# Three latent projections placed between the last normalisation's sums, later ones by token block, weight buffers rotated by one

## The chip, the core and the metric

One core of a Trainium2 chip runs the whole program. The metric is the device time of one execution in microseconds (us); for a kernel it is the median of several runs. TensorE does the matrix products, VectorE, ScalarE and GpSimd the elementwise work, SyncE issues the DMAs.

## The reference, cut to what matters

The program is a two-layer decoder trunk on 1024 tokens of width 1024. Each layer is a token mixer and a gated ConvFFN, each with an RMSNorm before it and one behind it. The change lies where layer 0's feed-forward ends and layer 1's mixer (DSA) begins:

```
def rms_norm(x, g):  y = x * rsqrt(mean(x*x) + eps);  return y * g
for i in range(2):
    x = x + rms_norm(mixer_i(rms_norm(x, g[i,0])), g[i,1])
    y = conv_ffn(rms_norm(x, g[i,2]), ...)
    x = x + rms_norm(y, g[i,3])
# layer 1's mixer:
proj = h @ w_in          # h = rms_norm(x, g[1,0]); w_in gives q, c, qi, ki, wi
c = rms_norm(c, kv_norm) # c: the latent, 256 wide
k = rope(c @ w_uk);  v = c @ w_uv
ki = rope(ki)            # the indexer's key, 64 wide; wi: 8 wide
```

So between the two layers stand two normalisations one behind the other: the "post" norm of the feed-forward's output, added to x, and the "pre" norm of the new x. Only then can layer 1's projections of these tokens start.

## The kernel before, in words

**Tiles.** Activations are held transposed: 128 rows of the width on the partitions, tokens along them, in two halves of 512 tokens (hf = 0 and 1). A float32 product is made of three matmuls with split operands (product, lines 493 to 495): high weights by high activations, high by low, low by high. HH and HL hold the high and the low part of the normalised activations, WH and WL those of a weight tile. One projection of one half (project) is 8 k-tiles by 3 matmuls = 24 matmuls of 128x512 into one PSUM bank.

**Weights.** SyncE loads a tile of 512 KB into one of two raw buffers WR, after the tile before it in this buffer has been split (load, line 450). It is split into one of three buffers WH/WL: in the feed-forward by ScalarE (WH, line 475) and VectorE (WL, line 482), in layer 1's first stage by GpSimd (split: a touch on line 462, WH on 463, WL on 466). A split waits until the matmuls of the tile that held its WH/WL buffer are done; the "done" pair given to plan.one() says what that is. Raw and split buffers are fixed by hand through their numbers in plan.one().

**End of the feed-forward.** The last group's down products are PE's last work in it (three output banks in turn; VectorE adds them into Y, line 1445). Half 0 was normalised many groups earlier, between the groups of the second half; half 1 comes at the very end. For half 1 (ffn_act, ffn_dve, last_norm_pe):
- post norm: ScalarE squares Y (L567), VectorE adds the squares (sum_dve, L598), PE sums over partitions with a matmul by ones into bank 7 (stat_pe, L647), ScalarE takes the root (L583), VectorE the reciprocal (L604) and then updates x in 8 tiles (L614, L620);
- pre norm: squares of x (L578), their sum (L598), the matmul by ones (L647), root, reciprocal, then 8 times product (L627), high part HH by ScalarE (L588), low part HL by VectorE (L635). n_hl[1] counts the HL tiles.

**Start of layer 1.** prep1_pe runs the latent projections LATENT_UNITS = [(0,0),(1,0),(2,0),(0,1),(1,1),(2,1),(3,0),(3,1)], pairs of (weight tile j, half). Tiles 0 and 1 are the latent c, 2 holds the indexer's key, 3 the key's and wi's last columns. I call them units 0 to 7 below. Unit x writes bank x % 4. Units 0, 1, 2 and 6 need half 0 alone. ScalarE (prep1_act) evicts them in order once both halves are normalised; unit 4 waits for unit 0's eviction, unit 5 for unit 1's, unit 6 for rot and t1 of unit 2. After unit 5 come the sums of the latent's squares (sums, L2124). VectorE's prep1_dve first sets memory, then does the rotary steps.

**SyncE's order** is one list: ffn_sp; prep1_loads (tiles c0 and c1); a wait until x is complete in both halves (residual, line 554's counter n_x); the store x_save (4 MB, line 2664); prep1_sp: tiles c2 and c3; a wait for both normalised halves; cosines, sines and constants; the next weight tiles. GpSimd's order is: split c0, c1, c2, c3, then the following tiles. Before the change c0 uses raw buffer 0 and split buffer 0, c1 1 and 1, c2 0 and 2, c3 1 and 0. The feed-forward's last three tiles (the last up tile, and the two down tiles of the last group) use raw 0, 1, 0 and split 2, 0, 1.

Of the kernel before, what the change touches and what calls it, by code (L numbers as in the profile page):

```python
# [26 lines left out]
DT = D // P  # L27
# [208 lines left out]
def trunk(nc, A, out):  # L236
    ctx = ExitStack()
    with ctx:
# [145 lines left out]
        def bank(b):  # L384
            return PS[:, b, :]
# [8 lines left out]
        plan = WeightPlan()  # L394
# [4 lines left out]
        k1_mm = semaphore("k1_mm")  # L399
        i_mm = semaphore("i_mm")  # L400
        proj = semaphore("a_proj")
# [5 lines left out]


        def attention_weights(n, infos, first):
            infos["q"] = [plan.one((first + m) % 2, (first + m) % 3, (proj, 16 * n + 2 * m + 2))  # L410
                          for m in range(PAIRS)]


            plan.last_done = [(qk, n * plans[0].NU + plans[n].ends[r] + 1)
                              for r in ((13, 14, 15), (15, 13, 14))[n]]
            infos["out"] = [plan.one((k + 1) % 2, (k + 1) % 3, (out_mm, 16 * n + k + 1))
                            for k in range(2 * DT)]
# [14 lines left out]
            return f  # L432
        F = [ffn_plan(0)]
        L1 = {}
        L1["c"] = [plan.one(n % 2, n % 3, (k1_mm, (4, 5, 6, 8)[n])) for n in range(4)]
        L1["i"] = [plan.one((4 + j) % 2, (4 + j) % 3, (i_mm, j + 1)) for j in range(4)]
        attention_weights(1, L1, 8)
        F.append(ffn_plan(1))
        w_raw = [semaphore("w_raw0"), semaphore("w_raw1")]
# [1 line left out]
        w_split = semaphore("w_split")  # L441
# [55 lines left out]
        def project(dst, info, hf, k0=0, k1=DT):  # L497

            wh, wl = weights(info)
            tok = slice(hf * HALF, (hf + 1) * HALF)  # L500
            for k in range(k0, k1):
                last = product(dst, wh[:, k, :], wl[:, k, :], HH[:, k, tok], HL[:, k, tok],
                               k == 0, k == DT - 1)
            return last


        def g_col(layer, which, dt):
# [17 lines left out]
        n_sq, n_acc, n_sum, n_root, n_rec, n_y, n_x, n_h, n_hh, n_hl = (  # L525
            [semaphore(f"n_{what}{hf}") for hf in range(2)]
            for what in ("sq", "acc", "sum", "root", "rec", "y", "x", "h", "hh", "hl"))
# [6 lines left out]
        for site in range(1, 5):  # L534
            layer_no, first = (site - 1) // 2, 1 if site % 2 else 3
# [9 lines left out]
        def tokens(hf):  # L545
            return slice(hf * HALF, (hf + 1) * HALF)

        def normalized(engine, hf, site):

            engine.wait_ge(n_hl[hf], 8 * (site + 1))  # L550
# [87 lines left out]
        def stat_pe(pe, site, kind, hf):  # L638
            b, k = site_buf[site], pass_no(site, kind)
            if (site, kind, hf) != (1, "post", 0):  # L640
                before = {("post", 0): (1, k - 1), ("pre", 0): (0, k - 1),
                          ("post", 1): (0, k + 1), ("pre", 1): (1, k - 1)}[kind, hf]
                if site == 4 and hf == 1:
                    before = (0, k)
                pe.wait_ge(n_root[before[0]], before[1] + 1)
            pe.wait_ge(n_acc[hf], summed(site, kind, 7))
            nc.tensor.matmul(bank(7), ONES[:, :], RT[b][:, hf, :], start=True,  # L647
                             stop=True).then_inc(n_sum[hf], 1)
# [908 lines left out]
                        low_dve(dve, 2, 1, dt - 1)  # L1557

        def last_norm_pe(pe, n):
            stat_pe(pe, 2 * n + 2, "post", 1)  # L1560
            if n == 0:
                stat_pe(pe, 2, "pre", 1)

        def ffn_sp(sp, n):
# [525 lines left out]
        def prep1_pool(pool):  # L2090
# [5 lines left out]
            for m in range(PAIRS):  # L2096
# [9 lines left out]
                if m >= 2:  # L2106
                    pool.wait_ge(a_saved[m % 2], a.saved0 + 32 * (m // 2))
                nc.gpsimd.tensor_tensor(query_part(1, m), QUERY, query_part(0, m).bitcast(F32),
                                        ALU.subtract).then_inc(a_qlo, 1)

        def prep1_pe(pe):
            S = sem1

            def transposes(v):
                for blk in range(4):
                    last = nc.tensor.transpose(PS[:, 4 + v % 2, blk * P:(blk + 1) * P],
                                               M["VT"][:, v % 2, blk * P:(blk + 1) * P], IDENT[:, :])
                last.then_inc(S["vtr"], 1)

            def sums():  # L2120
                pe.wait_ge(S["sq"], 4)
                for hf in range(2):
                    for c in range(2):
                        last = nc.tensor.matmul(bank(6 + hf), ONES[:, :], M["R"][:, c, tokens(hf)],  # L2124
                                                start=c == 0, stop=c == 1)
                    last.then_inc(S["sum"], 1)

            def queries(j, k0, k1):
                info = L1["i"][j]
                wh, wl = weights(info)  # L2130
                if k0 == 0:
                    pe.wait_ge(w_split, info["n"] + 1)
                    if j == 0:
                        pe.wait_ge(S["root"], 2)
                    else:
                        pe.wait_ge(S["rot"], (3, 4, 7)[j - 1])
                        pe.wait_ge(S["t1"], (3, 4, 7)[j - 1])
                for k in range(k0, k1):
                    for dst, tok in ((PS[:, 6, T - IQ:HALF], slice(T - IQ, HALF)),
                                     (bank(7), slice(HALF, T))):  # L2140
                        last = product(dst, wh[:, k, :], wl[:, k, :], HH[:, k, tok], HL[:, k, tok],
                                       k == 0, k == DT - 1)
                if k1 == DT:
                    last.then_inc(i_mm, 1)

            def scores(j, n0, n1):
                pe.wait_ge(S["rl"], (3, 4, 7, 8)[j])
                for n in range(n0, n1):
                    i, h = 2 + n // 2, n % 2
                    b0 = 2 * (n % 2)  # L2150
                    if 12 * j + n >= 2:
                        pe.wait_ge(S["rel"], 12 * j + n - 1)
                    for c in range((i + 4) // 4):
                        w = min(4, i + 1 - 4 * c) * P
                        q = M["QS"][:, j % 2, h, (i - 2) * P:(i - 1) * P]
                        keys = slice(c * HALF, c * HALF + w)
                        nc.tensor.matmul(PS[:, b0 + c, 0:w], q, M["KIH"][:, keys], start=True, stop=False)
                        last = nc.tensor.matmul(PS[:, b0 + c, 0:w], q, M["KIL"][:, keys], start=False,
                                                stop=True)
                    last.then_inc(S["sc"], 1)  # L2160

            for x, (j, hf) in enumerate(LATENT_UNITS):
                pe.wait_ge(w_split, L1["c"][j]["n"] + 1)
                normalized(pe, hf, 2)
                if x == 6:
                    pe.wait_ge(S["rot"], 1)
                    pe.wait_ge(S["t1"], 1)
                elif x >= 4:
                    pe.wait_ge(S["ev"], (1, 2, 0, 3)[x - 4])
                project(bank(x % 4), L1["c"][j], hf).then_inc(k1_mm, 1)  # L2170
                if x == 5:
                    sums()
            for v in range(2):
                pe.wait_ge(S["ev"], 5 + v)
                transposes(v)
            queries(0, 0, DT)
            queries(1, 0, 4)
            for n in range(12):
                scores(0, n, n + 1)
                if n < 4:  # L2180
                    queries(1, 4 + n, 5 + n)

            pe.wait_ge(S["vdone"], 2)
            pe.wait_ge(S["wl"], 1)
            pe.wait_ge(S["cl"], 1)
            for hf in range(2):
                for c in range(2):
                    last = product(bank(4 + hf), M["WKVH"][:, c, :], M["WKVL"][:, c, :],
                                   M["CH"][:, c, tokens(hf)], M["CL"][:, c, tokens(hf)], c == 0, c == 1)
                last.then_inc(S["kv"], 1)  # L2190
            for n in range(12):
                scores(1, n, n + 1)
                if n < 8:
                    queries(2, n, n + 1)
            for hf in range(2):
                pe.wait_ge(S["ev"], 8)
                pe.wait_ge(S["rot"], 6)
                pe.wait_ge(S["t1"], 6)
                transposes(2 + hf)
            for n in range(12):  # L2200
                scores(2, n, n + 1)
                if n < 8:
                    queries(3, n, n + 1)
            scores(3, 0, 12)
            for k in range(ROUNDS):
                if k == 0:
                    pe.wait_ge(S["cn"], 3)
                    pe.wait_ge(S["t1"], 8)
                if k >= 4:
                    pe.wait_ge(a_rot, A1.q0 + k - 3)  # L2210
                project_queries_pe(pe, A1, k, 4 + k % 4)
# [629 lines left out]
```

## Time and profile before

| | us |
|---|---|
| median of 3 runs | 3223.09 |
| lowest and highest | 3220.22, 3223.22 |
| the profiled execution | 3217.6 |
| its span | 3215.8 |
| PE busy | 2945.4 (92%) |
| VectorE busy | 2045.8 (64%) |
| ScalarE busy | 1508.2 (47%) |
| GpSimd busy | 320.8 (10%) |
| mean granted clock of TensorE | 0.951 of full speed |

The page has one row of busy shares for each engine over 40 slices of 80.4 us; the place of the change is in slices 21 and 22, around 1673 to 1762 us from the span's start, where PE's digit falls from 9 to 7 and 8. There one reads the timeline: each line is an instruction or a run of equal ones with its start, its duration and, in brackets, how long its engine sat idle before it and what released it. PE's matmuls overlap in it, so their rate is the distance of two starts and not the duration printed.

### The profile page before, as it was taken

To read this page: it belongs to the slowest core of one execution; us is meant where nothing else is said; L and a number is where in the kernel's file an instruction comes from. 1 tells how busy PE (TensorE), PEld (TensorE's weight loads), DVE (VectorE), ACT (ScalarE), POOL (GpSimd) and SP (SyncE) were. 2 spreads that over 40 slices of the span, in tenths; PEclk is the share of its full clock that TensorE was granted. 3 is DMA by queue.
4 is the path that set the end of the run, shared out by engine and by line. 5 is a ranking of instruction groups with operands and counts; after the bars stand their busy time and mean duration, and the time that the engine had idled before them with its cause. 6 is when DMAs were issued, how large, how long until landed. Compare 5 with 4: busy or idle time off the path is not lost.

```text
span 3215.8 us, 35590 instructions
## 1 busy us (share of the span) xinstructions
PE 2945.4 (92%) x12424; PEld 2224.0 (69%) x12424; DVE 2045.8 (64%) x3635; ACT 1508.2 (47%) x2614; POOL 320.8 (10%) x255
## 2 busy tenths in 40 slices
PE   7797999999999999999987776579999999999997
PEld 5685655655677888878866654345577788887885
DVE  6545545555377776677766789654427777667666
ACT  4333555555354444445433556444435454444443
POOL 2253000000300000000012124130030000000000
PEclk9878999999999999999998888689999999999998
DMA  5144121121433333333323013341143333332332
GB/s 172 40 98 122 41 60 42 45 53 39 125 95 92 92 98 92 99 92 92 99 65 119 1 53 109 101 133 47 34 132 92 92 98 92 99 96 88 108 99 76
DMA packets 356618, 275.05 MB, mean 86 GB/s; under 512 B 58085, under 2 KB 308007, under 8 KB 355927
## 3 DMA queue, kind: packets, MB, share of 16 engines
q1 hardware_dynamic: 355287, 270.68, 28.9%
q8 instruction: 99, 1.62, 0.2%
q10 hardware_dynamic: 1152, 2.10, 0.2%
q14 instruction: 80, 0.66, 0.1%
HBM read 238.18 MB, written 31.92 MB: 84 GB/s over the span
## 4 chain that ended last, share of the span: by engine, by line
PE 76%; DVE 10%; DMA 5%; ACT 3%; issue 3%; SPq 2%; POOL 1%; DVEq 0%; ACTq 0%; POOLq 0%
PE PS L493 19%; PE PS L495 19%; PE PS L494 19%; PE PS L929 8%; PE PS L841 3%; PE PS L904 2%; PE PS L905 2%; PE PS L910 1%; DMA r_save<-n_R 1%; DMA n_RB<-r_save 1%; DMA n_R<-n_DR 1%; DVE m_MASK L2391 1%; DVE m_Z L2465 1%; PE PS L647 0%; DMA m_ROT<-m_QF 0%
## 5 line engine op out<-in xcount | busy, mean ns | idle before, releaser
L493 PE MATMUL PS<-HH,WH 128*128 128x512 f32 (+1 forms) x2160 | 853.8, 395 | 48.6 <-POOL WL L466 22.8
L494 PE MATMUL PS<-HL,WH 128*128 128x512 f32 (+1 forms) x2160 | 846.0, 392 | 0.0
L495 PE MATMUL PS<-HH,WL 128*128 128x512 f32 (+1 forms) x2160 | 845.6, 391 | 0.0
L493 PEld LDWEIGHTS PS<-HH,WH 128*128 128x128 f32 x2160 | 411.9, 191 | 142.2 <-issue 44.5
L494 PEld LDWEIGHTS PS<-HL,WH 128*128 128x128 f32 x2160 | 412.1, 191 | 85.0 <-issue 2.0
L495 PEld LDWEIGHTS PS<-HH,WL 128*128 128x128 f32 x2160 | 411.0, 190 | 85.8
L482 DVE TENSOR_TENSOR WL<-WR,WH 128x1024 fp32r<-128x1024 f32 x280 | 341.8, 1221 | 46.9 <-ACT WH L475 42.5
L475 ACT ACTIVATE WH<-WR 128x1024 fp32r<-128x1024 f32 x280 | 297.6, 1063 | 115.5 <-PE PS L495 90.1
L949 ACT ACTIVATE n_PX<-PS 128x512 f32<-128x512 f32 (+1 forms) x320 | 172.8, 544 | 218.6 <-PE PS L910 110.9
L1053 DVE CUSTOM_DVE_ANT_0 n_JUNK<-PS,n_MZ 128x512 bf16<-128x512 f32 (+2 forms) x320 | 147.2, 487 | 103.6 <-PE PS L841 103.6
L462 POOL TENSOR_TENSOR TOUCH<-WR 128x1 f32<-128x1 f32 x55 | 16.5, 301 | 1784.9 <-PE PS L495 984.0
L1445 DVE TENSOR_TENSOR Y_c<-PS,Y_c 128x512 f32<-128x512 f32 x160 | 106.9, 687 | 89.4 <-PE PS L495 89.0
L1445 DVE TENSOR_TENSOR Y_b<-PS,Y_b 128x512 f32<-128x512 f32 x160 | 106.9, 688 | 87.3 <-PE PS L495 86.8
L929 PE MATMUL PS<-m_PX,m_V 128*128 128x512 f32 (+1 forms) x320 | 158.1, 578 | 0.0
L929 PE MATMUL PS<-n_PX,n_VS 128*128 128x512 f32 (+1 forms) x320 | 155.1, 566 | 2.7 <-ACT n_OP L968 2.5
L1053 DVE CUSTOM_DVE_ANT_0 m_JUNK<-PS,m_MASK 128x512 bf16<-128x512 f32 (+3 forms) x160 | 89.5, 595 | 95.2 <-PE PS L841 94.8
L949 ACT ACTIVATE m_PX<-PS 128x512 f32<-128x512 f32 (+1 forms) x160 | 88.2, 553 | 131.7 <-PE PS L910 130.3
L493 PE MATMUL PS<-HIDH_b,WH 128*128 128x512 f32 x352 | 142.3, 404 | 6.3 <-issue 3.2
L493 PE MATMUL PS<-HIDH_c,WH 128*128 128x512 f32 x352 | 142.5, 405 | 3.9 <-issue 3.2
L494 PE MATMUL PS<-HIDL_b,WH 128*128 128x512 f32 x352 | 139.9, 397 | 0.0
L495 PE MATMUL PS<-HIDH_b,WL 128*128 128x512 f32 x352 | 139.8, 397 | 0.0
L495 PE MATMUL PS<-HIDH_c,WL 128*128 128x512 f32 x352 | 139.7, 397 | 0.0
(374 smaller groups left out, 5188.8 us busy)
## 6 DMA issues: line engine op xcount, KB each, us to landing
WR<-in_ffn_w_up SPq DMA_DIRECT2D x176, 512.0 KB, 3.8
WR<-in_ffn_w_down SPq DMA_DIRECT2D x88, 512.0 KB, 3.7
WH<-qh_save SPq DMA_DIRECT2D x64, 256.0 KB
n_RB<-r_save SPq DMA_DIRECT2D x96, 128.0 KB, 3.1
WL<-ql_save SPq DMA_DIRECT2D x32, 256.0 KB
WR<-in_nsa_w_out SPq DMA_DIRECT2D x16, 512.0 KB, 4.8
WR<-in_dsa_w_in SPq DMA_DIRECT2D x16, 512.0 KB, 4.5
WR<-in_dsa_w_out SPq DMA_DIRECT2D x16, 512.0 KB, 4.3
```

Source lines behind the costliest of these rows:

```text
L475: nc.scalar.activation(WH[:, x, :], WR[:, r, :], ACT.Copy).then_inc(w_hi, 1)
L482: nc.vector.tensor_tensor(WL[:, x, :], WR[:, r, :], WH[:, x, :].bitcast(F32), ALU.subtract).then_inc(w_split, 1)
L493: nc.tensor.matmul(dst, wh, xh, start=start, stop=False)
L494: nc.tensor.matmul(dst, wh, xl, start=False, stop=False)
L495: return nc.tensor.matmul(dst, wl, xh, start=False, stop=stop)
L841: last = nc.tensor.matmul(PS[:, ring_bank(a, y), 0:w], query_high(a, p.r, p.h, p.ii * P, P), KA[:, g, k0:k0 + w], start=True, stop=True)
L904: nc.tensor.matmul(dst, KA[:, g, keys], both_heads(a, WH, n), start=True, stop=False)
L905: last = nc.tensor.matmul(dst, KB[:, g, keys], both_heads(a, WL, n), start=False, stop=not masks)
L929: last = nc.tensor.matmul(dst, V[:, g, n.kb, :], both_parts(B["PX"][:, u % 4, :], n), start=n.first, stop=n.last)
L949: nc.scalar.activation(a.B["PX"][:, u % 4, 0:2 * n.w], PS[:, u % 3, 0:2 * n.w], ACT.Exp).then_inc(a_ex, 1)
L1053: nc.vector.tensor_tensor_reduce(out=B["JUNK"][:, x % 2, 0:w], in0=src, in1=mask, scale=1.0, scalar=-3e38, op0=ALU.add, op1=ALU.max, accum ...
L1445: nc.vector.tensor_tensor(y, bank(4 + x % 3), y, ALU.add).then_inc(f.da, 1)
```

## The change

The latent projections move into one function, latent_units_pe. Unit 0 is issued ahead of the matmul by ones of the post norm of half 1, units 1 and 2 between it and that of the pre norm, units 3 to 7 where they were. Each unit now waits for the HL tiles of its half one by one, ahead of the three matmuls that use it, where before it waited for all eight. Since c0's weights are wanted as soon as the feed-forward's last product is issued, the raw and split buffers of c0 to c3, of the four index tiles and of layer 1's query tiles move on by one: c0 has raw 1 and split 2, c1 0 and 0, c2 1 and 1, c3 0 and 2. Nothing in SyncE's, GpSimd's, ScalarE's and VectorE's order changes.

```diff
--- before.py
+++ after.py
@@ -407,7 +407,7 @@
 
 
         def attention_weights(n, infos, first):
-            infos["q"] = [plan.one((first + m) % 2, (first + m) % 3, (proj, 16 * n + 2 * m + 2))
+            infos["q"] = [plan.one((first + m + n) % 2, (first + m + 2 * n) % 3, (proj, 16 * n + 2 * m + 2))
                           for m in range(PAIRS)]
 
 
@@ -432,8 +432,8 @@
             return f
         F = [ffn_plan(0)]
         L1 = {}
-        L1["c"] = [plan.one(n % 2, n % 3, (k1_mm, (4, 5, 6, 8)[n])) for n in range(4)]
-        L1["i"] = [plan.one((4 + j) % 2, (4 + j) % 3, (i_mm, j + 1)) for j in range(4)]
+        L1["c"] = [plan.one((n + 1) % 2, (n + 2) % 3, (k1_mm, (4, 5, 6, 8)[n])) for n in range(4)]
+        L1["i"] = [plan.one((5 + j) % 2, (6 + j) % 3, (i_mm, j + 1)) for j in range(4)]
         attention_weights(1, L1, 8)
         F.append(ffn_plan(1))
         w_raw = [semaphore("w_raw0"), semaphore("w_raw1")]
@@ -1557,8 +1557,11 @@
                         low_dve(dve, 2, 1, dt - 1)
 
         def last_norm_pe(pe, n):
+            if n == 0:
+                latent_units_pe(pe, 0, 1)
             stat_pe(pe, 2 * n + 2, "post", 1)
             if n == 0:
+                latent_units_pe(pe, 1, 3)
                 stat_pe(pe, 2, "pre", 1)
 
         def ffn_sp(sp, n):
@@ -2108,6 +2111,21 @@
                 nc.gpsimd.tensor_tensor(query_part(1, m), QUERY, query_part(0, m).bitcast(F32),
                                         ALU.subtract).then_inc(a_qlo, 1)
 
+        def latent_units_pe(pe, x0, x1):
+            S = sem1
+            for x in range(x0, x1):
+                j, hf = LATENT_UNITS[x]
+                pe.wait_ge(w_split, L1["c"][j]["n"] + 1)
+                if x == 6:
+                    pe.wait_ge(S["rot"], 1)
+                    pe.wait_ge(S["t1"], 1)
+                elif x >= 4:
+                    pe.wait_ge(S["ev"], (1, 2, 0, 3)[x - 4])
+                for k in range(DT):
+                    pe.wait_ge(n_hl[hf], 8 * 2 + k + 1)
+                    last = project(bank(x % 4), L1["c"][j], hf, k, k + 1)
+                last.then_inc(k1_mm, 1)
+
         def prep1_pe(pe):
             S = sem1
 
@@ -2159,17 +2177,9 @@
                                                 stop=True)
                     last.then_inc(S["sc"], 1)
 
-            for x, (j, hf) in enumerate(LATENT_UNITS):
-                pe.wait_ge(w_split, L1["c"][j]["n"] + 1)
-                normalized(pe, hf, 2)
-                if x == 6:
-                    pe.wait_ge(S["rot"], 1)
-                    pe.wait_ge(S["t1"], 1)
-                elif x >= 4:
-                    pe.wait_ge(S["ev"], (1, 2, 0, 3)[x - 4])
-                project(bank(x % 4), L1["c"][j], hf).then_inc(k1_mm, 1)
-                if x == 5:
-                    sums()
+            latent_units_pe(pe, 3, 6)
+            sums()
+            latent_units_pe(pe, 6, 8)
             for v in range(2):
                 pe.wait_ge(S["ev"], 5 + v)
                 transposes(v)
```

## Rows read from the trace of the kernel before

**Rows 1.** The page, part 4: lines that carry the chain that ended last.
```profile
PE PS L493 19%; PE PS L495 19%; PE PS L494 19%; PE PS L929 8%; PE PS L841 3%; PE PS L904 2%; PE PS L905 2%; PE PS L910 1%; DMA r_save<-n_R 1%; DMA n_RB<-r_save 1%; DMA n_R<-n_DR 1%; DVE m_MASK L2391 1%; DVE m_Z L2465 1%; PE PS L647 0%; DMA m_ROT<-m_QF 0%
```

**Rows 2.** Busy time by stretch: start:end, length, PE, PEld, DVE, ACT, POOL, clock, DMA.
```profile
1698.00:1703.00 5.00, 1.37 (x3) 0.84 (x3) 3.07 (x5) 1.66 (x3) 0.00 (x0) 0.50 0.98 419
```

**Rows 3.** Timeline of PE, 1672 to 1767: start, duration, engine, line, what [idle, releaser].
```profile
1672.92 0.40 PE L495 MATMUL PS<-HIDH_b,WL 128*128 128x512 f32 x1
1679.72 2.04 PE L647 MATMUL PS<-RT_b,ONES 128*128 128x512 f32 x2 [6.40 <-DVE RT_b L598]
1701.63 2.05 PE L647 MATMUL PS<-RT_b,ONES 128*128 128x512 f32 x2 [19.87 <-DVE RT_b L598]
...
1715.03 0.46 PE L493 MATMUL PS<-HH,WH 128*128 128x512 f32 x1
...
1721.48 0.47 PE L493 MATMUL PS<-HH,WH 128*128 128x512 f32 x1 [0.76 <-DVE HL L635]
...
1727.04 0.39 PE L493 MATMUL PS<-HH,WH 128*128 128x512 f32 x1
...
1766.68 0.55 PE L493 MATMUL PS<-HH,WH 128*128 128x256 f32 x1 [4.51 <-DVE m_QF L2435]
```

**Rows 4.** The same timeline of PE at the last down products, after 3 us idle.
```profile
1660.31 0.69 PE L493 MATMUL PS<-HIDH_b,WH 128*128 128x512 f32 x1 [3.06 <-DVE HIDL_b L1433]
...
1664.06 0.39 PE L493 MATMUL PS<-HIDH_b,WH 128*128 128x512 f32 x1
```

**Rows 5.** Line 647 in the whole trace: min/median/max ns of one matmul.
```profile
L647 PE MATMUL PS<-RT_b,ONES x16: 592/592/1193, 886.4 to 1702.6; 128*128 128x512 f32 x16
```

**Rows 6.** Timeline of POOL, 1673 to 1732.
```profile
1674.78 2.65 POOL L466 TENSOR_TENSOR WL<-WR,WH 128x1024 fp32r<-128x1024 f32 x1
...
1712.23 2.71 POOL L466 TENSOR_TENSOR WL<-WR,WH 128x1024 fp32r<-128x1024 f32 x1
1727.35 0.20 POOL L462 TENSOR_TENSOR TOUCH<-WR 128x1 f32<-128x1 f32 x1 [12.41 <-PE PS L495]
...
1728.64 2.39 POOL L466 TENSOR_TENSOR WL<-WR,WH 128x1024 fp32r<-128x1024 f32 x1
```

**Rows 7.** The chain that ended last, 1675 to 1680: start, us, what.
```profile
1675.33 2.66 DVE RT_b L598
1678.08 1.50 DVE RT_b L598
```

**Rows 8.** Timeline of DVE, 1694 to 1732.
```profile
1694.82 1.28 DVE L620 TENSOR_TENSOR XT_b<-XT_b,Y_b 128x512 f32<-128x512 f32 x2
...
1711.15 1.54 DVE L627 SCALAR_TENSOR_TENSOR SQ_b<-XT_b,COLS,RT_b 128x512 f32<-128x512 f32 x1
1712.61 2.88 DVE L635 TENSOR_TENSOR HL<-SQ_b,HH 128x512 fp32r<-128x512 f32 x1
1715.41 0.74 DVE L627 SCALAR_TENSOR_TENSOR SQ_b<-XT_b,COLS,RT_b 128x512 f32<-128x512 f32 x1
...
1719.87 1.47 DVE L635 TENSOR_TENSOR HL<-SQ_b,HH 128x512 fp32r<-128x512 f32 x2
...
1731.82 0.69 DVE L2435 SCALAR_TENSOR_TENSOR m_QF<-PS,m_COS 128x512 f32<-128x512 f32 x1
```

**Rows 9.** Timeline of ACT at the first eviction of a latent unit.
```profile
1722.00 0.59 ACT L2274 ACTIVATE m_C<-PS 128x512 f32<-128x512 f32 x1
```

**Rows 10.** Timeline of SyncE's queue, 1696 to 1706: issues.
```profile
1696.18 0.34 SPq L2664 DMA_DIRECT2D x_save<-XT_b  x1
1696.57 8.78 SPq L450 DMA_DIRECT2D WR<-in_dsa_w_in  x2
```

**Rows 11.** DMA issues, 1696 to 1697: count, KB, us from issue to landing.
```profile
x_save<-XT_b SPq DMA_DIRECT2D x1, 4096.0 KB, 12.1
WR<-in_dsa_w_in SPq DMA_DIRECT2D x1, 512.0 KB, 13.5
```

**Rows 12.** Weight tile loads landing, 1690 to 1740: us to landing, min/median/max.
```profile
DMA to landing us min/median/max: 3.7/4.9/15.7
```

## The prediction

> **What bounds the kernel now.** I read the chain by line first: over half of it is the three matmul lines of the projections [rows 1], so in most of the program PE is the bound and a microsecond that PE loses there is lost for good. The seam between the two layers is different. The window before the pre sum shows PE almost empty, at a granted clock of 0.50 [rows 2], which is the 1.2 GHz level. The timeline of PE says why: the last down product starts at 1672.92, the post sum (L647) at 1679.72 after 6.40 us idle, the pre sum at 1701.63 after 19.87 us idle, both released by VectorE's adds [rows 3]. Here a serial chain of VectorE and ScalarE steps sets the pace: adds, post sum, root, reciprocal, eight updates of x, adds, pre sum, root, reciprocal, eight tiles of HH and HL.
>
> What PE does behind the pre sum matters most. Units 0, 1 and 2 run from there to about 1720.7, and unit 3 starts at 1721.48 after 0.76 us idle, released by the last HL [rows 3]. So **the three units that are moved are hidden already**, under the pre norm's reciprocal and HL tiles. Moving them earlier gives nothing by itself; what can be won is unit 3 running along with the HL tiles, and some warmth and quiet. From 1721.48 PE has no gap until the 4.51 us before 1766.68 [rows 3]; that gap is released by a rotary step behind an eviction behind PE's own product. So a shift of PE at unit 4 goes through to the end, one for one.
>
> **The wait that is added.** Unit 2 needs weight tile c2. SyncE issues c2's load only after x is complete and after the 4 MB store x_save: the store at 1696.18, the load at 1696.57 [rows 10]. It takes 13.5 us to land, where the store takes 12.1 [rows 11], so it comes out behind the store. GpSimd starts on it when it lands, at 1710.1, and ends at 1712.23 + 2.71 = 1714.94, and unit 2 starts at 1715.03 [rows 3, 6]. The change leaves the list of SyncE as it is, but puts unit 2 ahead of the pre sum, which before started at 1701.63. PE's queue is in order: what is queued behind unit 2's wait is the pre sum, and for that wait the whole rest of the norm, on ScalarE and VectorE. This is the main term.
>
> **The sum, step by step,** on the profiled execution's time axis.
>
> 1. *c0 earlier.* With split buffer 2, last read by the last up tile, GpSimd can split c0 while the last down products run. That puts its work beside VectorE's HIDL step, on which PE waits until 1660.31 [rows 4]. An op of VectorE beside a GpSimd split can grow: 2.88 us for one HL tile where two take 1.47 elsewhere [rows 8], which bounds the cost by 2.1 us. I take nothing, since GpSimd must wait for the last split of the feed-forward, which VectorE does just before HIDL, and then reads a touch first. Ahead of the post sum the move gives something: of VectorE's last adds one took 2.66 us beside c0's split (WL at 1674.78) and the next 1.50 us beside the second split [rows 6, 7]. Now only one split (c1's) is there, so the last add takes about 0.7: minus 0.8 us, and the adds end at 1678.8.
> The Trainium skill, page "SBUF — State Buffer", section "Who interferes with whom", says that a VectorE op with two SBUF inputs and a GpSimd op that reads SBUF lock each other out for a whole instruction, whoever comes first. The stretched rows agree, and by it HIDL, which starts first, would lose nothing.
>
> 2. *Unit 0 ahead of the post sum.* 24 matmuls; the warm rate is read from unit 3: from 1721.48 to 1727.04 it takes 5.56 us in all, 0.23 each [rows 3]. From 1673.15 unit 0 ends at 1678.7, just as the adds end: hidden, and PE stays warm. The post sum took 2.04 us after 6.40 us idle [rows 3]; one of its two matmuls lasts 592 ns warm against 1193 [rows 5], so I take half, 1.0. It ends at 1680.0 instead of 1681.8: **minus 1.8** up to here. If unit 0 ran long it would cost what it overhangs.
>
> 3. *Unit 1* needs c1, split at about 1677.4 (2.65 from 1674.78 [rows 6], now c1's place). It runs from 1680 to 1685.6, beside VectorE's post norm. Free.
>
> 4. *The wait for c2.* x is complete at 1694.82 + 1.28 = 1696.1 [rows 8], now 1694.3. Store and load follow 1.8 earlier, c2 lands at about 1708.3. A split undisturbed by VectorE takes 1728.64 + 2.39 − 1727.35 = 3.7 us [rows 6] (4.8 from 1710.1, beside VectorE's norm): ready at 1712.0. PE has been idle since 1685.6, so unit 2 starts at the 1.2 GHz level. How long that lasts, a restart shows: from 1660.31 the durations printed are 0.63 to 0.69, and at 1664.06 they are back at 0.39, after 3.75 us and 9 matmuls [rows 4]. So 9 matmuls take 3.75 and the other 15 take 3.45 at the warm rate: 7.2 us (all warm 5.5, all cold, at 0.42 each, 10.1). Unit 2 ends at 1719.2, the pre sum, warm, at 1720.2. Before it ended at 1703.7: **plus 16.5**.
>
> 5. *The rest of the norm* keeps its steps, but c2's split no longer falls into it. Before, the product step at 1711.15 took 1.54 and the HL step behind it 2.88, where others take 0.74 and 0.73 (1.47 for two) [rows 8]: 0.8 + 2.15, **minus 3.0**. The last HL ends at 1719.87 + 1.47 = 1721.3 [rows 8] + 16.5 − 3.0 = 1734.8.
>
> 6. *Unit 3 by token block.* It starts with the first HL and takes three matmuls for each, at 0.7 us warm or 1.3 cold for every 1.4 us or less of VectorE (a product and an HL step), so it ends within 0.7 to 1.3 us of the last HL instead of 5.6. But unit 4 writes unit 0's bank, and ScalarE evicts it only after both halves are normalised: before, that eviction ended at 1722.00 + 0.59 = 1722.59, 1.25 us behind the last HL [rows 8, 9]. So unit 4 starts at 1736.1. Before, at 1727.04 [rows 3]: **plus 9.1**.
>
> 7. *Behind it.* VectorE and ScalarE are 13.5 us later, PE 9.1. Does this bind? Unit 6 needs the first rotary product, before at 1731.82 [rows 8], now at about 1745.3 to 1746; unit 6 stands behind unit 4, unit 5 and the sums, at least 11 us behind unit 4's start, so after 1747. It doesn't. c3, the index tiles and the query tiles rotate with the same distances. The waits for each HL tile stand in front of matmuls that queue behind others and I take nothing for them.
>
> Sum: plus 9.1. Span 3215.8 → 3224.9, profiled time 3217.6 → 3226.7. That execution lies 5.5 us under the median, 3223.1; on the median the forecast is **3232.2 us**, slower by 0.28%.
>
> **Bounds.** Down: unit 2 all warm −1.6, a landing two us sooner −2: plus 5.5, that is 3228.6. Up: unit 2 all cold +2.9, the slow split +1.1, HIDL disturbed +2.1, a cold start of units 4 and 5 +1.8: plus 17.0, 3240.1, with all at once unlikely. About 0.2% (6.4 us) is what a measurement of this kernel can tell from no change.
>
> **Rivals.**
> *A, c2 lands soon.* The load isn't held behind the store's bytes. A weight tile takes 3.7 us at best [rows 12]; then c2 is ready at 1694.7 + 3.7 + 3.7 = 1702.1, unit 2 ends at 1709.3, the pre sum at 1710.3, 6.6 later than before; less 3.0 and with step 6's end, unit 4 starts at 1726.2: minus 0.8, 3222 us. Against it: the same two issues, 0.4 us apart, took 12.1 and 13.5 us [rows 11], with DMA 0.98 busy [rows 2]. 0.09. The Trainium skill, page "DMA: Bandwidth & Descriptors", section "Queues, rings and completion order", has each DMA engine take descriptors in ring order; both are on one queue, so by it c2 stays behind the store, as in the rows.
> *B, faster.* The price of unit 2's wait is nil: its weights are there before VectorE's adds for the pre sum are, at 1701.6 − 1.8. Then the pre sum isn't delayed, the last HL is at 1721.3 − 1.8 − 3.0 = 1716.5 and unit 4 at 1717.8, minus 9.2: 3214 us. This decides as soon as c2 is ready before about 1694, with time for unit 2. It needs a load issued ahead of the store, and the list has none. What speaks for it is that the idle time is really there [rows 2]. 0.05.
> *C, absorbed.* The delay of PE at unit 4 is paid from slack in the score loops, where PE waits for others (4.51 us at 1766.68 [rows 3]). At most that much comes off: plus 4.6, 3227.7. Against it, the one released by VectorE hangs on PE's own product. 0.07.
> *D, colder.* PE drops to the lower level more often, as at 1660 after only 3 us idle [rows 4]: unit 2 all cold, and units 4 and 5 started cold, +5 on the forecast: plus 14, 3237. 0.11.
>
> **How the numbers follow.** The forecast's case has 0.68, of which 0.03 lies within 0.2%. Slower: 0.65 + 0.11 = 0.76. Within: 0.09 + 0.07 + 0.03 = 0.19. Faster: 0.05. The range runs from 3225, a little under C's end and the lower bound with the runs' scatter of some 3 us, to 3239, over D: it leaves out A, B and the far end of the sum.
>
> **What would show it.** In the profile after: unit 0's matmuls straight behind the last down product, the post sum at about 1679 with 1.0 us; unit 1 behind it; then PE idle for some 26 us, released by GpSimd's WL, and unit 2 at about 1712; the pre sum at about 1719 to 1720, VectorE idle before the root for some 20 us; the last HL near 1735 and unit 4 near 1736. SyncE's store still ahead of c2's load. The prediction is wrong if unit 2 starts before 1700, if unit 4 starts before 1730, or if PE's later gaps shrink by the delay.

## The result

The changed kernel took 3233.7 us in the median (3232.5 to 3237.6, 6 runs); the kernel before, over its first runs and those beside the changed one, 3218.7 us (3215.7 to 3223.2, 6 runs). The ratio is 1.0047, 95% interval 1.0034 to 1.006: slower by 15 us. The forecast was 3232.2 us from a base of 3223.1, plus 9.1 us. The sign, the place and the time hold; the size of the change does not: plus 15 where plus 9.1 stood, with an interval of 11 to 19. That the time itself comes within 1.5 us is in part luck: the base was 4.4 us lower than the one forecast from, and the change 5.9 us larger. Two further measurements of the same pair gave 1.0033 (1.0021 to 1.0046) and 1.0049 (1.0033 to 1.0064). In the later measurements five executions of four kernels took 3641 to 16507 us, far above all others; they enter no ratio.

The chain that ended last in the profile after, over the seam (start, us, what):

```profile
1681.62 0.70 ACT RT_b L583
1682.34 3.36 DVE RT_b L604
...
1694.72 1.22 DVE XT_b L620 x2
1696.38 13.54 DMA WR<-in_dsa_w_in
1710.18 1.02 POOL WH L463
1711.27 2.35 POOL WL L466
1713.67 0.80 PE PS L493
...
1721.39 0.87 PE PS L647 x2
1722.28 0.70 ACT RT_b L583
1723.00 3.37 DVE RT_b L604
```

The reader should see a DMA and two GpSimd steps in a chain that before had none of them there: from 1696.38 to 1713.6 the chain runs through weight tile c2. PE's timeline after, against [rows 3]:

```profile
1680.48 1.10 PE L647 MATMUL PS<-RT_b,ONES 128*128 128x512 f32 x2 [0.20 <-DVE RT_b L598]
...
1713.67 0.80 PE L493 MATMUL PS<-HH,WH 128*128 128x512 f32 x1 [26.64 <-POOL WL L466]
...
1721.22 1.02 PE L647 MATMUL PS<-RT_b,ONES 128*128 128x512 f32 x2
1728.68 0.76 PE L493 MATMUL PS<-HH,WH 128*128 128x512 f32 x1 [6.43 <-DVE HL L635]
...
1738.26 0.47 PE L493 MATMUL PS<-HH,WH 128*128 128x512 f32 x1 [0.34 <-issue]
```

Unit 2 starts after 26.64 us idle, released by c2's WL. The pre sum follows at 1721.22, where it stood at 1701.63. Unit 3 starts with the first HL tile at 1728.68, and unit 4 at 1738.26 instead of 1727.04, which is 11.2 us later; 1.5 of them were there already at the end of the down products. SyncE's issues are as before [rows 10], the store ahead of c2:

```profile
1696.00 0.34 SPq L2674 DMA_DIRECT2D x_save<-XT_b  x1
1696.38 8.76 SPq L450 DMA_DIRECT2D WR<-in_dsa_w_in  x2
```

And VectorE waits where before it had 2.95 us (timeline of DVE, before and after):

```profile
1704.44 3.35 DVE L604 RECIPROCAL RT_b<-RT_b 128x512 f32<-128x512 f32 x1 [2.95 <-ACT RT_b L583]
```
```profile
1723.00 3.35 DVE L604 RECIPROCAL RT_b<-RT_b 128x512 f32<-128x512 f32 x1 [21.70 <-ACT RT_b L583]
```

### The profile page after: what moved, and what is told of

Same layout as the page of the kernel before. It is cut to its first block, busy times and chain, and to the rows that moved or that the text cites. A ratio compares the mean times of both kernels' runs of the same rounds, so it can differ in the third digit from the quotient of the medians.

```text
span 3231.3 us, 35590 instructions
## 1 busy us (share of the span) xinstructions
PE 2951.7 (91%) x12424; PEld 2229.1 (69%) x12424; DVE 2040.0 (63%) x3635; ACT 1507.8 (47%) x2614; POOL 318.5 (10%) x255
## 4 chain that ended last, share of the span: by engine, by line
PE 77%; DVE 9%; DMA 4%; ACT 3%; issue 3%; SPq 2%; POOL 2%; DVEq 0%; ACTq 0%; POOLq 0%
PE PS L493 19%; PE PS L494 19%; PE PS L495 19%; PE PS L929 9%; PE PS L841 3%; PE PS L904 2%; PE PS L905 2%; PE PS L910 1%; DVE m_MASK L2401 1%; DMA n_R<-n_DR 1%; DMA r_save<-n_R 1%; DVE m_Z L2475 1%; DMA n_RB<-r_save 1%; DMA m_RB<-r_save 1%; DMA m_ROT<-m_QF 0%
## 5 line engine op out<-in xcount | busy, mean ns | idle before, releaser
L1445 DVE TENSOR_TENSOR Y_c<-PS,Y_c 128x512 f32<-128x512 f32 x160 | 106.9, 687 | 89.6 <-PE PS L495 89.2
L1445 DVE TENSOR_TENSOR Y_b<-PS,Y_b 128x512 f32<-128x512 f32 x160 | 106.9, 688 | 88.5 <-PE PS L495 88.1
```

The lines of the kernel that those rows point to most:

```text
L1445: nc.vector.tensor_tensor(y, bank(4 + x % 3), y, ALU.add).then_inc(f.da, 1)
```

## How the traces are compared

The total is a poor witness here: the kernel before varied from 3207 to 3225 us over the sessions, and the traces of the kernels differ by up to 7 us already ahead of the seam, where the program is the same. So I cut the seam at instructions of VectorE, whose order is the same in all kernels, and take the time between two starts. The marks are: (a) the last HIDL step, L1433; (b) the last add into Y, L1445; (c) the post norm's reciprocal, L604; (d) the first add of the pre norm's squares, L598; (e) the pre norm's reciprocal; (f) the last HL tile, L635; (g) the first copy of WI, columns of the last latent product, just behind the transposes (after the latent stage); (h) the first threshold count. Cold and warm stand for TensorE's 1.2 and 2.4 GHz levels. Each entry is read from one trace; "before" has two traces, the changed kernel three, the one with c2 early two.

| us | a-b last down products | b-c adds, post sum | c-d post norm | d-e adds, pre sum | e-f HL tiles | f-g latents | g-h scores |
|---|---|---|---|---|---|---|---|
| before | 13.8, 15.0 | 9.2, 9.2 | 13.5 | 8.4, 8.4 | 16.2 | 36.9 | 118.2, 119.2 |
| changed | 15.0, 13.8, 15.0 | 7.5 (all) | 13.5 | 27.2, 26.8, 27.2 | 13.2 | 32.7 | 119.5, 119.2, 119.5 |
| e1 unit 2 back | 12.2 | 7.5 | 13.5 | 8.4 | 16.1 | 38.3 | 118.4 |
| e2, e8 c2 early | 15.1, 13.8 | 8.3, 8.3 | 13.5 | 8.4, 8.4 | 13.2 | 32.7 | 119.9, 119.3 |
| e3 c2 before store | 13.8 | 7.5 | 13.5 | 18.9 | 13.2 | 32.7 | 119.9 |
| e4 blocks only | 13.8 | 9.2 | 13.5 | 8.4 | 16.2 | 35.9 | 119.1 |
| e5 rotation only | 12.2 | 8.3 | 13.5 | 8.4 | 16.2 | 36.9 | 118.5 |
| e9 no blocks | 13.7 | 7.5 | 13.5 | 28.1 | 13.2 | 39.6 | 119.8 |

## The experiments

The theory is that of the prediction: unit 2 stands ahead of the pre sum in PE's order, its weights come behind a 4 MB store, and the norm waits. Rival 1 is that the rotated buffers cost, since GpSimd splits c0 beside the last down products; rival 2 that the moved units leave PE colder.

**e1: unit 2 alone back behind the pre sum.** In last_norm_pe and prep1_pe of the changed kernel:

```diff
-                latent_units_pe(pe, 1, 3)
+                latent_units_pe(pe, 1, 2)
...
-            latent_units_pe(pe, 3, 6)
+            latent_units_pe(pe, 2, 6)
```

> The changed kernel with unit 2 alone put back behind the pre sum; unit 0 stays ahead of the post sum, unit 1 between the sums. Theory (unit 2's wait for c2 holds the pre sum): the pre sum starts at about 1701 again, c2's split again falls beside the norm's tiles, unit 2 runs from 1714 to 1721 and unit 4 starts at 1726 to 1727, so the time is that of the kernel before, within -2 to +1 us. Rival 1 (the buffers' rotation costs, c0's split beside the last down products): 10 us or more over the kernel before stay. Rival 2 (PE's colder clock after the moved units costs): most of the 15 us stay too.

Measured: ratio 1.0000 to before (0.9989 to 1.0012), 11 runs. PE's timeline:

```profile
1693.95 2.04 PE L647 MATMUL PS<-RT_b,ONES 128*128 128x512 f32 x2 [14.42 <-DVE RT_b L598]
1707.24 0.80 PE L493 MATMUL PS<-HH,WH 128*128 128x512 f32 x1 [11.24 <-POOL WL L466]
```

The pre sum is released by VectorE's adds again, and only unit 2 waits for GpSimd. Moving one unit takes the whole loss away, with buffers, unit 0, unit 1 and the waits by block still in place. Rival 1 as the main cause falls; for rival 2, e2 below keeps PE's whole order and loses nothing either. The gain of the earlier post sum (-1.7) is given back: unit 2 starts cold, so unit 3 does too late what it could do with the HL tiles (f-g 38.3).

**e5: the rotated buffers alone, on the kernel before.**

```diff
-        L1["c"] = [plan.one(n % 2, n % 3, (k1_mm, (4, 5, 6, 8)[n])) for n in range(4)]
+        L1["c"] = [plan.one((n + 1) % 2, (n + 2) % 3, (k1_mm, (4, 5, 6, 8)[n])) for n in range(4)]
...
```

> The kernel before with the rotated weight buffers alone. Theory: c0 is split beside the last down products; one split less beside VectorE's last adds, the post sum 0.8 us sooner: 0 to -1 us. If c0's split disturbs the down phase (it was 1.2 us longer in the changed kernel's trace), +1 to +2. Rival 1: +10 or more.

Measured: 1.0002 (0.9992 to 1.0012). b-c falls from 9.2 to 8.3, the 0.8 us of step 1. a-b is the shortest of all, 12.2, though c0's split lies beside it. So this split disturbs nothing, and the 1.2 us that the changed kernel's first trace had over before's there has another cause. The windows name it (start:end, length, PE, PEld, DVE, ACT, POOL, clock, DMA), e5 first:

```profile
1653.00:1658.00 5.00, 4.63 (x20) 3.77 (x21) 1.83 (x4) 1.26 (x2) 3.78 (x3) 1.00 0.40 105
```

the changed kernel:

```profile
1660.00:1665.00 5.00, 4.37 (x10) 3.47 (x11) 1.27 (x2) 0.63 (x1) 3.96 (x3) 0.50 0.39 105
1665.00:1670.00 5.00, 5.00 (x19) 3.95 (x18) 2.11 (x4) 0.63 (x1) 0.00 (x0) 0.83 0.00 0
```

and the kernel before:

```profile
1660.00:1665.00 5.00, 4.69 (x14) 3.69 (x15) 0.99 (x3) 0.63 (x1) 0.00 (x0) 0.66 0.81 210
```

In all three PE sat idle for 3.06 us before it. One came back at 2.4 GHz, one at 1.2 GHz for 3.75 us [rows 4], one for 6.1. The stretch takes 12.2, 13.8 or 15.0 us accordingly, and the kernel before shows both of the latter in its two traces.

**e2: c2's load issued behind c1's, ahead of the wait for x and the store.**

```diff
-            for j, col in enumerate((1024, 1152)):
+            for j, col in enumerate((1024, 1152, 1728)):
                 load(sp, L1["c"][j], columns("dsa_w_in", col), DT)
...
-            for j, col in ((2, 1728), (3, 1736)):
+            for j, col in ((3, 1736),):
```

> The changed kernel with c2's load issued right behind c1's, ahead of the wait for x and of the store. Theory: units 1 and 2 both end before VectorE's adds for the pre sum, at about 1692; the pre sum starts at 1700 to 1701, the last HL is at 1716 to 1718, unit 4 starts at about 1718: 8 to 10 us faster than the kernel before, some 24 us faster than the changed one. Rivals 1 and 2: still slower than the kernel before, since the buffers, the order of PE and its idle times are those of the changed kernel.

Measured: 0.9994 (0.9985 to 1.0003), 11 runs. In PE's timeline the pre sum is back to VectorE's pace, and unit 4 is at 1717.57:

```profile
1699.51 2.04 PE L647 MATMUL PS<-RT_b,ONES 128*128 128x512 f32 x2 [8.95 <-DVE RT_b L598]
1707.99 0.76 PE L493 MATMUL PS<-HH,WH 128*128 128x512 f32 x1 [6.43 <-DVE HL L635]
...
1717.57 0.47 PE L493 MATMUL PS<-HH,WH 128*128 128x512 f32 x1 [0.34 <-issue]
```

The mechanism came as expected, the gain did not: the seam's terms b to g add up to -8.1 us, while the time fell by 2. e8 below takes this up.

**e3: c2's load behind the wait for x, but ahead of the store.** load(c2) stands one line above the store and is taken out of prep1_sp.

```diff
+            load(sp, L1["c"][2], columns("dsa_w_in", 1728), DT)
             sp.dma_start(x_save, XT[1][:, :, :]).then_inc(saved, 16)
```

> The changed kernel with c2's load still behind the wait for x, but ahead of the 4 MB store: only the store's bytes are taken out of c2's way. Theory: c2 lands about 4 us after its issue instead of 13.6, unit 2 starts at 1702 to 1703, the pre sum at about 1709, unit 4 at 1726 to 1727: the time of the kernel before within 2 us, that is two thirds of e2's gain over the changed kernel. If the wait for x is what counts and not the store, it stays at +10 or more over the kernel before.

Measured: 1.0016 (1.0008 to 1.0025). SyncE and GpSimd:

```profile
1691.27 0.37 SPq L450 DMA_DIRECT2D WR<-in_dsa_w_in  x1
1691.68 0.58 SPq L2675 DMA_DIRECT2D x_save<-XT_b  x1
```
```profile
1695.75 0.20 POOL L462 TENSOR_TENSOR TOUCH<-WR 128x1 f32<-128x1 f32 x1 [21.48 <-DMA WR<-in_dsa_w_in]
```

c2 is there 4.5 us after its issue instead of 13.6. The stretch d-e is 18.9 us, 10.5 over before's 8.4, where the changed kernel has 18.6 over it: the store's bytes make 8.1, and the late issue, the split and the cold unit 2 the other 10.5. So rival A of the prediction priced a real dependence, and the order on one queue decides it. The seam's terms add up to +1.6, near what I expected; the time is +5 and not within 2, a miss.

**e4: the waits by token block alone, on the kernel before.** In prep1_pe the wait for all eight HL tiles becomes one ahead of each k-tile.

```diff
-                normalized(pe, hf, 2)
...
-                project(bank(x % 4), L1["c"][j], hf).then_inc(k1_mm, 1)
+                for k in range(DT):
+                    pe.wait_ge(n_hl[hf], 8 * 2 + k + 1)
+                    last = project(bank(x % 4), L1["c"][j], hf, k, k + 1)
+                last.then_inc(k1_mm, 1)
```

> The kernel before with the waits for each HL tile alone. Units 0 to 2 keep PE busy until 1720.7, where the last HL is at 1721.3: unit 3 can run ahead by under 1 us. Theory: seam 0 to -1 us, time the same. If waiting by block were what costs, or what gives, it would differ by more.

Measured: 1.0000 (0.9989 to 1.0012), f-g 35.9 instead of 36.9. As expected: with units 0 to 2 behind the pre sum PE has hardly a gap to run ahead in.

**e9: the changed kernel without these waits.** The reverse edit in latent_units_pe.

```diff
-                for k in range(DT):
-                    pe.wait_ge(n_hl[hf], 8 * 2 + k + 1)
-                    last = project(bank(x % 4), L1["c"][j], hf, k, k + 1)
-                last.then_inc(k1_mm, 1)
+                normalized(pe, hf, 2)
+                project(bank(x % 4), L1["c"][j], hf).then_inc(k1_mm, 1)
```

> The changed kernel without the waits by token block: each unit waits for all eight HL tiles of its half. Theory: unit 3 starts behind the last HL instead of ahead of it and takes 5.5 us or more (cold again after 14 us idle: 7 to 9), so the stretch from the last HL tile to the first transposes is back at 36.9 us or 1 to 3 over, where the changed kernel has 32.7: 4 to 7 us slower than the changed kernel. Rival: ScalarE's eviction of unit 0 hides it, and it costs under 1 us.

Measured: 1.0071 (1.0056 to 1.0086) to before, against 1.0049 of the changed kernel beside it; f-g is 39.6 instead of 32.7.

```profile
1733.90 0.77 PE L493 MATMUL PS<-HH,WH 128*128 128x512 f32 x1 [14.80 <-DVE HL L635]
```

Unit 3 starts behind the last HL, after 14.80 us of idle time, and cold. So the waits by block are worth 6.9 us once the other units are out of the way, and 1.0 us when they are not (e4): the same edit, two prices. (The 0.9 us more in d-e are unit 2's: its matmuls were cold for 6.1 us in this trace, against 4.3 in the changed kernel's first.)

**e6, e7, e8, e10, e11: repeats.** The seam's terms b to g explain 9.5 to 9.8 of the 15 us, and e2's trace lost 8.6 us again behind the seam. Is that the change or chance?

> The kernel before once more, for a second trace. The theory is that the seam (from the last down products' start at L1433's HIDL to the transposes of the latent stage) repeats within 2 us of 92.8, since only the clock's level in the last down products can move it, and that stages before and behind it move by up to some us with the granted clock alone. A rival is that each kernel repeats its later stages closely, so that the 4 us that the changed kernel lost behind the seam belong to the change.

The second trace of the kernel before has 99.2 us from a to g where the first had 98.0 (the clock in a-b), and a total 3.8 us longer. Where it lost is the same place as in e2: in the start of layer 1's attention, some 290 us behind the seam. VectorE and PE there in the first trace:

```profile
2047.97 1.02 PE L929 MATMUL PS<-m_PX,m_V 128*128 128x512 f32 x2
...
2054.45 0.89 DVE L2420 SCALAR_TENSOR_TENSOR m_E<-m_R,m_NEED,m_E 128x640 f32<-128x640 f32 x1
```

and in the second trace of the same kernel:

```profile
2045.81 1.92 PE L929 MATMUL PS<-m_PX,m_V 128*128 128x512 f32 x2
...
2054.71 1.70 DVE L2420 SCALAR_TENSOR_TENSOR m_E<-m_R,m_NEED,m_E 128x640 f32<-128x640 f32 x1
```

In both traces PE's granted clock is 0.50 for 10 us and more ahead of this place. In the first it is back at 1.00 from about 2046, in the second some 7 us later, when both are counted from the first threshold count (a pair of matmuls takes 1.92 instead of 1.02 us). That costs 2.7 us, and then two of VectorE's mask steps meet GpSimd's rotary steps and take 1.70 and 1.76 us instead of 0.89 each. Together 4.4 us. It hit the second trace of before, e2, e3, e4, e7, e9 and e10, and not the first of before, e1, e5, the changed kernel's first and e8: no kernel with two traces or more has it always.

> The changed kernel once more. Theory: the seam is again 102 to 104 us, 9 to 11 over before; from the score loops on (1780 to 3200 us of before) the loss is anything from 0 to 6 us with the clock's level in the places where PE is idle half the time. Rival: again close to +4.1 there. Ratio to before 1.003 to 1.006 by either.

Measured: 1.0033 (1.0021 to 1.0046), plus 10.6 us. d-e is 26.8 and f-g 32.7, as in the first trace. Behind g this trace lies 7.1 us over the first trace of before, more than the 6 I allowed, but 0.2 under the second one: both of these have the long cold spell at the attention's start. From a to the end the two differ by 8.1 us: b to g by +9.5, a-b by -1.2, the rest by -0.2. In this pair nothing beyond the seam's terms is left over.

> The changed kernel with c2's load ahead of the store once more. Its seam was 6.9 us shorter than before's, yet its time was only 2 us under (interval -5 to +1), since its trace lost 8.6 us behind the seam, 4.5 of them at 2044 to 2056 us with PE at the lower clock there. Theory (chance): that loss isn't repeated at the same places, and over all runs the gain is 3 to 7 us. Rival (the loss is its own): the same places lose again, gain 0 to 3 us.

Measured: 0.998 (0.997 to 0.999), minus 6.4 by the ratio; its trace didn't have the 4.4 us. Of my own two theories, chance fits this one.

> The changed kernel a third time, beside e9 and e11 on one chip, for a better interval. The seam's terms give +9.6 us; the two measurements gave +15.1 and +10.6. Theory (the rest is the clock's chance): 8 to 13 over before. Rival (a cost of its own behind the seam): 13 to 17 again.

Measured: 1.0049 (1.0033 to 1.0064), plus 16: outside the 8 to 13 that I put for chance alone and in the rival's 13 to 17, though the interval, 11 to 21, covers part of both.

> The changed kernel with c2's load ahead of the store a third time. The seam's terms give -8.1 us, the two measurements gave -2 and -6. Theory: 4 to 9 under before. Rival (a cost of its own behind the seam, of some 4 us): 2 to 5 under.

Measured: 0.9982 (0.9971 to 0.9994), minus 5.8. That is in the theory's 4 to 9, and the interval, 2 to 9, covers the rival's 2 to 5 too. Its trace is of an execution of 11406 us and isn't used. Over the three measurements c2 early is 0.06, 0.20 and 0.18% under the kernel before, two of the intervals clear of one: about 5 us faster than before and 18 faster than the changed kernel. It is the version to keep.

## Why the prediction was right, and where its size was off

- **Units 0 to 2 were hidden already** (what bounds the kernel). Held: with unit 2 back, e1 equals the kernel before.
- **Steps 1 and 2**, the earlier c0, unit 0 and the warm post sum, forecast -0.8 and -1.0. Measured in b-c: 9.2 to 7.5, -1.7; the rotation alone gives 0.8 of it (e5). The bound of 2.1 us for HIDL was not needed: nothing was lost there. HIDL took 0.68 us before and after, and GpSimd's touch, which began 0.16 us behind it, took 0.57 us, where the next one takes 0.19:

```profile
1659.89 0.68 DVE L1433 TENSOR_TENSOR HIDL_b<-CV_b,HIDH_b 128x512 fp32r<-128x512 f32 x1
```
```profile
1660.05 0.57 POOL L462 TENSOR_TENSOR TOUCH<-WR 128x1 f32<-128x1 f32 x1 [787.07 <-DVE WL L482]
```

By the Trainium skill, page "SBUF — State Buffer", section "Who interferes with whom", the order of issue decides which of two such instructions blocks; the trace agrees.

- **Step 4**, the wait. Forecast: from -1.8 at the post sum to +16.5 at the pre sum, 18.3 us in all. Measured in d-e: 18.4 to 18.8. In the first trace unit 2's matmuls were at the 1.2 GHz level for 4.3 us instead of 3.75.
- **Step 5**, c2's split out of the norm: forecast -3.0, measured 16.2 to 13.2, -3.0.
- **Step 6**, unit 3 with the HL tiles and unit 4 at ScalarE's pace: forecast 13.5 at the last HL to 9.1, -4.4. Measured 36.9 to 32.7, -4.2.
- **Step 7 and the sum.** Forecast +9.1 through to the end. The terms measured give -1.7 + 18.6 - 3.0 - 4.2 = +9.7. The mechanism was right and each of its terms within 0.5 us; what is off is the last step, which carried the seam's sum to the end as if nothing else moved. Three measurements of the total gave +15, +11 and +16, a mean of 14, some 4 us more than the terms.

What these 4 us are is settled only in part. The first trace of the changed kernel is 15.5 us longer than before's first: 0.3 ahead of the seam, 1.2 in a-b (the clock), 9.8 from b to g, 1.4 in the score loops and 2.7 behind them. For the clock in a-b and the 4.4 us at the attention's start the repeats show that the level changes from one execution of a kernel to the next: the kernel before has both. They don't show that it falls equally often to either side: the long cold spell at the attention hit five of the seven traces with the three units ahead of the pre sum and two of the other five, and a-b is 14.3 us on average in the seven and 13.4 in the five. For the score loops they show less. All seven traces of kernels with the three units ahead of the pre sum (changed, e2, e3, e8, e7, e10, e9) have 119.2 to 119.9 us in g-h, all five of the others (before twice, e1, e4, e5) 118.2 to 119.2. That is 0.9 us on average and may be the change's own, though the two groups touch, the second trace of before and e4's come within 0.2 us of the seven, and no instruction there differs; I have no experiment that shows how. With these averages (9.7, 0.9 in a-b, 0.9 in g-h, and 4.4 us in three traces of ten more, 1.4) one comes to about 13 of the 14 us. Whether the cold levels come more often with this order or fell so by chance, twelve traces can't tell. And the kernels with c2 early, whose terms give -8.1, came out at -2, -6.4 and -5.8, again some 3 us worse than their terms. So the step is known and its cause isn't: a cost of about 1 to 4 us outside the seam's terms, which may go with this order, stays open.

**Rivals.** A (c2 lands soon) had the mechanism, as e3 shows, and not the condition: the store goes first, and c2 lands 13.5 us after its issue. The Trainium skill, page "DMA: Bandwidth & Descriptors", section "Queues, rings and completion order", has each DMA engine take descriptors in ring order; both orders of the two issues agree with it, 4.5 us with the load first and 13.6 with the store first. B (faster, c2 in time) is what e2 builds: its seam is 8.1 us shorter where 9.2 were forecast, the rest being the second split beside the adds (8.3 instead of 7.5 in b-c). C (absorbed): nothing was absorbed; the gap of 4.51 us at 1766.68 is 4.51 again after, at 1778.02. D (colder) forecast plus 14, which is the size measured, but by another mechanism than the traces show: unit 2 was cold for 4.3 us and not for all of its time, and unit 4 started warm. What there is of it is the cold spell of 6.1 us at the last down products, which the kernel before shows too, and the 4.4 us above.

## What to carry to other kernels

An in-order engine makes a filler dangerous: work put into its idle time must have all its inputs by then, its weights' load, split and queue place included, or what stands behind it waits too. Before moving a step up, follow each of its inputs back through the queue that issues it; here the edit without and with the change of the load's place (two lines) differ by 18 us. And when a seam is compared, cut it at instructions of an engine whose order hasn't changed: the terms from b to g then repeat within 0.4 us where the total scatters by 10 and more. Compare more than one trace of each kernel, too: the stretches on either side of them moved by 1 to 4 us in the same kernel.

## What the runs showed of the hardware

- After the same 3.06 us of idle time TensorE stayed at 2.4 GHz in two traces (e1, e5), was at 1.2 GHz for 3 to 4 us in six (in two of these, e3 and e7, only from about 1 us behind the restart) and for 6.1 us in four (the changed kernel's first, e2, e6, e10): a stretch of 12.2, 13.8 or 15.0 us of the same program.
- A spell at the 1.2 GHz level that lasted some 7 us longer at the beginning of layer 1's attention cost 4.4 us, 1.7 of them because two steps of VectorE that had slipped then lay beside GpSimd's (1.70 and 1.76 instead of 0.89 us).
- A load of 512 KB issued 0.4 us ahead of a 4 MB store was usable after 4.5 us; issued 0.4 us behind it, after 13.6 us.
